# FFN up projection: order of VectorE's and ScalarE's work around the change from whole products to seven block products

## The reference, cut to what matters

```python
def conv_ffn(h, w_up, conv_w, conv_b, w_down):
    u = h @ w_up                                   # 1024 x 5632, f32
    up = pad(u, two rows in front)
    u = sum(up[:, i:i + T] * conv_w[i] for i in range(3)) + conv_b
    gate, val = split(u, 2)                        # 2816 each
    return (gelu(gate) * val) @ w_down
```

## Time and profile before

| what | value |
|---|---|
| median of 3 runs | 2358.38 us (2356.68 to 2360.41) |
| profiled execution, its own time | 2357.89 us |
| span of the profile | 2356.1 us |
| granted TensorE clock, mean | 0.996 of full speed |
| PE busy | 2308.7 us (98%) |
| DVE busy | 1409.2 us (60%) |
| ACT busy | 758.0 us (32%) |
| POOL busy | 918.5 us (39%) |

### The profile page before, as it was taken

The page is one execution under the profiler, slowest core; times in us unless marked ns, Lnnn a source line. Parts: engine busy times, 40 slices in busy tenths (PEclk is TensorE's granted clock), DMA queues, the critical chain, the costliest instruction groups (busy, mean ns, idle before and its releaser), DMA issues.

```text
span 2356.1 us, 33483 instructions
## 1 busy us (share of the span) xinstructions
PE 2308.7 (98%) x12752; PEld 1880.9 (80%) x12752; DVE 1409.2 (60%) x1641; ACT 758.0 (32%) x1253; POOL 918.5 (39%) x545
## 2 busy tenths in 40 slices
PE   7999999999999999999999989999999999999998
PEld 6788888888888888888877867888878887777776
DVE  7755374537543754576538885555541487757775
ACT  4311131112112211334225234444432445114442
POOL 3311231123112214312466467777734445422164
PEclk9999999999999999999999999999999999999999
DMA  3211211121111114664453422222246433211123
GB/s 146 79 54 46 73 54 57 51 73 58 51 55 63 63 54 125 204 200 151 171 161 127 168 89 81 81 81 83 85 164 209 139 123 98 70 59 38 35 81 117
DMA packets 71175, 230.67 MB, mean 98 GB/s; under 512 B 6785, under 2 KB 11009, under 8 KB 70401
## 3 DMA queue, kind: packets, MB, share of 16 engines
q1 hardware_dynamic: 40560, 138.76, 18.2%
q10 hardware_dynamic: 30480, 89.97, 10.4%
HBM read 182.04 MB, written 46.66 MB: 97 GB/s over the span
## 4 chain that ended last, share of the span: by engine, by line
PE 89%; DVE 5%; ACT 2%; issue 1%; POOL 1%; DVEq 1%; DMA 1%; POOLq 1%; ACTq 0%; SPq 0%
PE psg L763 7%; PE psg L768 6%; PE psg L770 6%; PE psg L631 3%; PE psg L636 3%; PE psg L635 3%; PE psa L1235 3%; PE psa L1237 3%; PE psa L1238 3%; PE psb L1237 2%; PE psb L1235 2%; PE psb L1238 2%; PE psg L725 2%; PE psg L728 2%; PE psg L729 2%; PE psa L863 1%
## 5 line engine op out<-in xcount | busy, mean ns | idle before, releaser
L520 POOL CAST whi<-wraw 128x1024 fp32r<-128x1024 f32 (+1 forms) x142 | 158.2, 1114 | 1113.4 <-PE psg L763 516.6
L522 POOL TENSOR_TENSOR wlo<-wraw,whi 128x1024 fp32r<-128x1024 f32 (+1 forms) x142 | 361.4, 2545 | 20.5 <-issue 0.2
L763 PE MATMUL psg<-xhi,whi 128*128 128x512 f32 x640 | 260.9, 408 | 0.0
L770 PE MATMUL psg<-xhi,wlo 128*128 128x512 f32 x640 | 259.5, 406 | 0.0
L768 PE MATMUL psg<-xlo,whi 128*128 128x512 f32 x640 | 257.2, 402 | 0.0
L631 PE MATMUL psg<-xhi,whi 128*128 128x512 f32 x464 | 185.3, 399 | 2.0 <-issue 1.9
L636 PE MATMUL psg<-xhi,wlo 128*128 128x512 f32 x464 | 183.4, 395 | 0.0
L635 PE MATMUL psg<-xlo,whi 128*128 128x512 f32 x464 | 182.8, 394 | 0.0
L595 POOL TENSOR_TENSOR wlo<-wraw,whi 128x1024 fp32r<-128x1024 f32 (+1 forms) x50 | 112.0, 2241 | 146.6 <-ACT whi L2778 78.5
L763 PEld LDWEIGHTS psg<-xhi,whi 128*128 128x128 f32 x640 | 120.9, 189 | 26.8 <-issue 6.3
L770 PEld LDWEIGHTS psg<-xhi,wlo 128*128 128x128 f32 x640 | 120.8, 189 | 22.6 <-issue 1.0
(11 more groups left out here) (706 smaller groups left out, 5992.0 us busy)
## 6 DMA issues: line engine op xcount, KB each, us to landing
wraw<-w SPq DMA_DIRECT2D x206, 512.0 KB, 3.5
later_scratch<-stage ACTq DMA_DIRECT2D x40, 512.0 KB, 2.6
sraw<-w SPq DMA_DIRECT2D x18, 512.0 KB, 4.1
ff_scratch<-ring ACTq DMA_DIRECT2D x10, 512.0 KB, 2.6
ff_scratch<-ff ACTq DMA_DIRECT2D x10, 512.0 KB, 2.6
ff<-ff_scratch ACTq DMA_DIRECT2D x5, 1024.0 KB, 7.0
xres<-xt ACTq DMA_DIRECT2D x4, 1024.0 KB, 11.1
RV<-later_scratch SPq DMA_DIRECT2D x4, 1024.0 KB, 11.3
```

The source lines that it names most:

```text
L520: pool.tensor_copy(whi[:, u, 0:width], wraw[:, u, 0:width])
L522: pool.tensor_tensor(wlo[:, u, 0:width], wraw[:, u, 0:width], whi[:, u, 0:width].bitcast(F32), ALU.subtract).then_inc(w_ready, 1)
L763: mm = pe.matmul(ps[:, cols], whi[:, slot, w_cols], xhi[:, k, cols], start=(k == 0), stop=False)
L770: mm = pe.matmul(ps[:, cols], wlo[:, slot, w_cols], xhi[:, k, cols], start=False, stop=(k == KT - 1))
```

## The change

Arithmetic and outputs stay as they are. What changes:

- DVE's `hidden` is split in `take`, `plain_taps` and `hidden_made`, and the calls are written out. DVE takes pair 4 and makes the last token lows ahead of the taps and the hidden product of pair 3. The taps of pair 4 are made between `gate_first` and `gate_last` of pair 5.
- Pair 4 is taken in place: its scaled raw value stays in `psg`. For pair 5, whose sums went to `psg`, `fg` and `fv` row 1 take that place (`gate_raw`, `value_raw` at `WHOLE`).
- The order of pair 5's sums becomes 22, 11, 12, 21 (`summed`), and its gate taps follow its value taps at once, ahead of the sums of pair 6.
- The copy of the constants to `cp` and its semaphore are gone: operations read them from `prm`. A semaphore `halves_in` takes over the order for pair 1.
- ACT casts the four token highs ahead of P6's high part, keeps P1 right after it, and makes gelu of pair 3 after P5, P7, P4 and P3's high parts and keep P6. Gate of pair 4, the write of pair 3's hidden tile, and value of pair 4 come after keep P7.
- At the start of the down projection ACT makes the high part of the second weight block ahead of that of hidden tile 1, and the last gelu after the fourth hidden tile and weight block.

The diff, cut to its core:

```diff
 def summed(c, i):
-    return 4 * (i - WHOLE) + (22, 11, 21, 12).index(c) + 1
+    order = (22, 11, 12, 21) if i == WHOLE else (22, 11, 21, 12)
+    return 4 * (i - WHOLE) + order.index(c) + 1
...
         def gate_raw(i):
-            return fg[:, 1, :] if i == FT - 1 else psg[0][:, :]
+            return fg[:, 1, :] if i in (WHOLE, FT - 1) else psg[0][:, :]
...
+        def plain_raw(i):
+            if i == 1:
+                return fg2, fv2
+            return (psg[0], psg[1]) if i == WHOLE - 1 else (fg[:, 1, :], fv[:, 1, :])
...
+            def take(i, u):
+                v.drain()
+                v.wait_ge(g_full, T_UP + 2 * i + u + 1)
+                tt(plain_raw(i)[u][:, 0:T], psg[u][:, :], frs[:, :], MUL).then_inc(g_free[u], 1)
+
+            def plain_taps(i):
+                v.drain()
+                for u, buf in enumerate((fg, fv)):
+                    src = plain_raw(i)[u]
+                    v.wait_ge(sem("cv_a"), 2 * i + u + 1)
+                    stt(buf[:, 0, 1:T], src[:, 0:T - 1], conv_col(i, 4 * u + 1), buf[:, 0, 1:T], MUL, ADD)
+                    v.drain()
+                    stt(buf[:, 0, 2:T], src[:, 0:T - 2], conv_col(i, 4 * u), buf[:, 0, 2:T], MUL, ADD
+                        ).then_inc(sem("cv_taps"), 1)
...
-            hidden(3, middle=(1,), between=(2, 3))
-            hidden(4, lows=last_token_lows)
+            take(3, 0)
+            token_sums_of(1)
+            take(3, 1)
+            token_sums_of(2)
+            token_sums_of(3)
+            take(4, 0)
+            take(4, 1)
+            last_token_lows()
...
+            plain_taps(3)
+            hidden_made(3)
+            value_last(WHOLE)
+            gate_first(WHOLE)
+            plain_taps(4)
+            gate_last(WHOLE)
+            hidden_made(4)
+            value_first(WHOLE)
+            taps(WHOLE, 1, fv, value_raw(WHOLE))
+            taps(WHOLE, 0, fg, gate_raw(WHOLE))
...
                     weight_highs(2)
-                gelu(i)
-            weight_highs(3)
-            gate(WHOLE - 1)
-            put_hidden(WHOLE - 2)
+                else:
+                    gelu(i)
+            s.wait_ge(sem("t_raw"), since("t_raw", 4 * kh))
             s.wait_ge(g_full, T_UP + 2 * WHOLE)
             for k in range(kh):
                 act(xhi[:, k, HALF:T], t4raw[:, k, :], CP).then_inc(sem("t_high"), 1)
-            weight_highs(2)
-            value(WHOLE - 1)
+            weight_highs(1)
             keep("P1", WHOLE)
-            weight_highs(2)
-            gelu(WHOLE - 1)
+            weight_highs(4)
             keep("P6", WHOLE)
+            gelu(WHOLE - 2)
             weight_highs(2)
             s.wait_ge(sem("t_low"), since("t_low", 4 * kh))
             keep("P7", WHOLE)
-            weight_highs(1)
+            gate(WHOLE - 1)
+            put_hidden(WHOLE - 2)
+            value(WHOLE - 1)
+            weight_highs(3)
+            gelu(WHOLE - 1)
+            keep("P1", WHOLE + 1)
             put_hidden(WHOLE - 1)
-            keep("P1", WHOLE + 1)
             weight_highs(2)
             value_base(WHOLE)
...
+            s.wait_ge(sem("st_made"), since("st_made", len(PRODUCTS)))
+            weights_high(0, 0, 1)
             s.wait_ge(sem("gate_in"), since("gate_in", FT - WHOLE))
             hidden_high(0, 0, 1)
-            s.wait_ge(sem("st_made"), since("st_made", len(PRODUCTS)))
-            weights_high(0, 0, 1)
             gate_base(FT - 1)
             hidden_high(0, 1, 0)
             weights_high(0, 1, 0)
-            gate_gelu(FT - 1)
             hidden_high(0, 1, 1)
             weights_high(0, 1, 1)
+            gate_gelu(FT - 1)
```

More of the change, by code:

```diff
@@ L357, in gate_raw, with conv_col @@
         def gate_raw(i):
[L358 removed]
+            return fg[:, 1, :] if i in (WHOLE, FT - 1) else psg[0][:, :]
         def value_raw(i):
[L361 removed]
+            return fv[:, 1, :] if i in (WHOLE, FT - 1) else psg[1][:, :]
+        def plain_raw(i):
+            if i == 1:
+                return fg2, fv2
+            return (psg[0], psg[1]) if i == WHOLE - 1 else (fg[:, 1, :], fv[:, 1, :])
+        def conv_col(i, o):
+            return par_col("conv", 8 * i + o)
         dy = at("dy", x_at, [P, KT, T])
@@ L2066, in last_token_lows @@
                     tt(xlo[:, k, HALF:T], t4raw[:, k, :], xhi[:, k, HALF:T].bitcast(F32), SUB).then_inc(sem("t_low"), 1)
-            hidden(0, first=True)
+            plain_taps(0)
+            hidden_made(0)
             for q in range(2, AGAIN):
-                second_halves(q)
-            hidden(1, first=True)
-            hidden(2, between=(0,))
-            hidden(3, middle=(1,), between=(2, 3))
-            hidden(4, lows=last_token_lows)
-            def conv_col(i, o):
-                return par_col("conv", 8 * i + o)
+                second_halves(q).then_inc(sem("halves_in"), 1)
+            plain_taps(1)
+            hidden_made(1)
+            take(2, 0)
+            take(2, 1)
+            token_sums_of(0)
+            plain_taps(2)
+            hidden_made(2)
+            take(3, 0)
[6 more added lines that the diff above has]
+            last_token_lows()
             def value_last(i):
@@ L2114, in taps @@
                     mm.then_inc(sem("gate_taps"), 1)
[L2116 to L2127, removed]
+            plain_taps(3)
[8 more added lines that the diff above has]
+            taps(WHOLE, 0, fg, gate_raw(WHOLE))
+            for i in range(WHOLE + 1, FT):
+                if i > WHOLE + 1:
                     gate_last(i - 1)
@@ L2130, in _ @@
                 value_last(i)
-                if i > WHOLE:
-                    hidden_made(i - 1)
+                hidden_made(i - 1)
                 if i == FT - 1:
@@ L2750, in gate @@
                 s.wait_ge(sem("f_done"), i + 1)
-                s.wait_ge(sem("cp_ready"), i + 1)
                 s.wait_ge(g_free[0], T_UP // 2 + (3 if first else 2 + i))
-                act(fg[:, 0, :], fg2[:, :] if first and i else fg[:, 1, :], IDN, scale=cp[:, 2:3], bias=cp[:, 3:4]
+                if i == 1:
+                    s.wait_ge(sem("halves_in"), 1)
+                act(fg[:, 0, :], plain_raw(i)[0][:, 0:T], IDN, scale=conv_col(i, 2), bias=conv_col(i, 3)
                     ).then_inc(sem("cv_a"), 1)
@@ L2757, in value @@
                 s.wait_ge(g_free[1], T_UP // 2 + (3 if first else 2 + i))
-                act(fv[:, 0, :], fv2[:, :] if first and i else fv[:, 1, :], IDN, scale=cp[:, 6:7], bias=cp[:, 7:8]
+                if i == 1:
+                    s.wait_ge(sem("halves_in"), 2)
+                act(fv[:, 0, :], plain_raw(i)[1][:, 0:T], IDN, scale=conv_col(i, 6), bias=conv_col(i, 7)
                     ).then_inc(sem("cv_a"), 1)
```

21 lines of the change are left out of this document (4 added, 17 removed).

## The result

The changed kernel takes 2335.99 us (median of 4 runs, 2332.53 to 2337.02) against 2357.99 for the kernel before beside it: ratio 0.9903, 95% interval 0.9886 to 0.992. That is 22 us or 0.97% faster, where I had forecast 2.5 us. Some 20 of the 22 us come from a cause that the forecast did not contain: the removed tile `cp` moves other tiles by 32 bytes. The new order of work by itself gave 2.0 us, near the forecast, though not by all the steps that I had worked out.

What follows compares the result with a forecast made beforehand. PE, busy 98% of the span, was taken as the bound; 0 us from the block products' start plus 2.5 us from the down projection's start, off 2358.38, gave 2355.9 us, range 2351.0 to 2359.0.

Steps and rivals of the forecast that it cites:

- part 3: Small edits: removing the copies to cp and their semaphore, on DVE beside PE's work, was put at 0 us.
- my sum: Whole kernel: 0 us from the block products' start plus 2.5 us from the down projection's start, 2355.9 us.
- part 1: Start of the block products, new ACT and DVE order and pairs 4 and 5 moved: 1.7 - 1.8 = 0 us.
- P6 of pair 5: Block products: PE's wait of 9.7 us before it becomes 0.9 us, with no fall of the clock.
- P4 of pair 5, none: Block products: the 2.15 us wait before it goes; P3 of pair 5 then ends 13.5 us ahead, near 1407.0.
- P6 of pair 6, 4.5 us: Block products: a new PE wait of about 4.5 us, until 1411.6, behind POOL's sums and ACT's list.
- P4 of pair 6: Block products: starts at 1430.3 after a new wait of about 6 us, leaving 1.7 us of PE's lead.
- The clock, 1.8 us at P4 of pair 6: Clock falls after the roughly 6 us wait there, costing 1.8 us, bounds 0 and 2.2.
- Collisions: DVE operations with two SBUF inputs delay POOL: 0.85 us each for 11 wide, 0.42 for 5 narrow.
- The tail, 2.5 us: Start of the down projection: waits before second and fourth weight blocks go, 2.5 us saved, bounds 0 and 2.6.
- The rivals: POOL not held up by pair 5, 2351.5 (0.24); no down-projection gain, 2358.4 (0.16); slower from full blocking, 2362.1 (0.10).
- "Faster": Whole kernel: outcome faster by over 0.2%, under 2353.7 us, given chance 0.28.

Runs made afterwards that it cites:

- first experiment: Kernel before, with only cp's 32 bytes taken from an unused part of sm, so xhi, xlo and the arena lie 32 bytes lower: 2336.34 us, ratio 0.9913.
- second experiment: Changed kernel with 32 unused bytes ahead of xhi, so every tile behind is at its old address: 2354.89 us, ratio 0.9993.
- the tail: Kernel before with tiles 32 bytes lower, plus only the change's ACT list at the start of the down projection: 2333.76 us, ratio 0.9902.

## Why the prediction was wrong

**The missing term.** The step that failed is part 3: "The copies to `cp` (0.17 us and a drain each) are on DVE beside PE's work." (One of the five took 1.05 us in the trace, which changes nothing.) I costed the instructions that go, and put the tile that goes at nothing without a reason. The tile's 32 bytes sat ahead of `xhi`, `xlo` and the arena, and their distance to the weights went from 96 to 64 modulo 256. That is 20.6 us (first experiment), some eight times my forecast. The clock has no part in it: 0.996 to 0.997 before, 0.995 to 0.997 with the tiles moved. The rows of before don't show it, but the trace had a hint: the prediction's 0.233 us from one matmul to the next holds for products on x, while those of t1h and sform started every 0.227 us in the same trace. I did not ask where that difference came from.

**The order, against the kernel with the old addresses.** The second experiment measures my sum: forecast 2.5 us, measured 2.0 us with an interval from 0 up. By the traces the agreement is partly luck. The second experiment's kernel is 1.1 us ahead at P1 of pair 5, which the sum did not have; it loses 1.8 us from there to the down projection (346.5 us against 344.7), where part 1 said 0; and it gains 2.8 us in the down projection's first half. Step by step:

- *P6 of pair 5*: forecast a wait of 0.9 us without a fall of the clock. 0.5 us there. In the changed kernel itself it is 1.8 us in both profiles: PE is done with P2 9.2 us earlier than in the second experiment, and POOL's low is there only 7.9 us earlier. The clock fell behind it in one of the two profiles.
- *P4 of pair 5, none*: right, but one step beside it was missed. P1 of pair 6 waits for its low part (2.2 us, and 1.1 in the changed kernel), as POOL's list has P4 and P3 ahead of it while PE's has it first. So PE's lead at the end of P3 of pair 5, counted from P1 of pair 5, was 11.1 us and not 13.5.
- *P6 of pair 6, 4.5 us*: started 28.2 us after P1 of pair 5, forecast 27.6. The wait is shorter (2.6 us), by what was lost before it. The clock fell here too, and P6 took 4.35 us; as forecast, that cost nothing, since PE waits again.
- *P7 of pair 6*: none, as I had it. In the changed kernel, where P6 ran at full clock, there is one of 2.6 us that I had not seen: keep P6 stands behind the value base and gate base of pair 5.
- *P4 of pair 6*: forecast 1430.3 with a wait of about 6 us and ACT's keep P7 ahead of it. POOL's sums of pair 7 ended at 1427.2, forecast 1427.7. Counted from P1 of pair 5, PE is 1.0 us ahead here, and not 1.7. Timeline of the second experiment's PE:

```profile
1429.97 0.76 PE L1244 MATMUL psa<-xhi,whi 128*128 128x512 f32 x1 [5.91 <-ACT sthird L2850]
```

- *The clock, 1.8 us at P4 of pair 6*: P4 and P1 of pair 7 took 5.26 and 3.12 us in that trace in place of 2.8 each, so it cost 2.8 us. With the 1.0 us of lead this is the loss of 1.8. In the changed kernel's own trace the clock is low in the stretches behind the waits before P6 of pair 5 and before P4 of pair 6 (length, PE, PEld, DVE, ACT, POOL busy, clock, DMA, GB/s):

```profile
1381.00:1384.00 3.00, 2.67 (x7) 2.15 (x8) 2.93 (x2) 1.23 (x3) 3.00 (x3) 0.61 0.00 0
...
1420.00:1422.00 2.00, 0.00 (x0) 0.00 (x0) 0.00 (x0) 1.90 (x3) 1.26 (x2) 1.00 0.00 0
1422.00:1425.00 3.00, 2.17 (x5) 1.82 (x6) 1.98 (x3) 1.20 (x3) 2.58 (x3) 0.60 0.00 0
...
1427.00:1430.00 3.00, 3.00 (x15) 2.47 (x14) 1.37 (x2) 1.84 (x2) 2.56 (x2) 1.00 0.35 137
```

- *Collisions*: 2.0 to 2.3 us for each of pair 5's taps, as in the sum. What the change saves for pair 4 it gives back for pair 5. The Trainium skill (SBUF — State Buffer, "Who interferes with whom") states an exclusive lock, and says of VectorE's two-port modes that the other engine is blocked in full. By such a lock each meeting would cost the whole other operation; the new rows again show a pair in 2.0 to 2.3 us where the two alone take 1.28 and 1.3.
- *The tail, 2.5 us*: right in place and about in size (2.6 to 3.1). DVE's low of hidden tile 1, begun beside POOL's operation, took 2.02 us where one alone takes 0.68, and ended 0.56 us after POOL's. That one meeting is what such a lock would give. The margin sufficed.
- *The rivals*: none was it. "Faster" had 0.28, by another mechanism, so that it came true is luck.

Part 1 by itself, forecast near 0, is a loss: 1.8 us on the old addresses by the traces (0.6 by the times, the tail's 2.6 less the 2.0 measured), 2 to 3 us on the new ones. By the times alone both are within what the intervals allow for nothing. What stays open: why the pace goes by the distance of the two tiles in this uneven way, with what period, and why shifting wlo alone costs so little.

## What to carry to other kernels

A diff that removes or adds a small tile moves all tiles behind it. Where TensorE is the bound, compare the number of matmuls in a stretch without waits before anything else, and try a few distances between the moving and the stationary tiles: here the distance alone spread one kernel over 1.3% (2328.5 to 2358.5, the latter one run), some fifteen times the 2.0 us that this new order gave. When a wait on the bounding engine goes, follow the slowest list behind it (here POOL's) to the next products that need it: of 11.1 us of lead at the end of pair 5 in the second experiment, 1.0 was left at the start of the fifth product after it.

## What the runs showed of the hardware

- The start-to-start time of matmuls of 128x128 by 512 columns depends on where in SBUF the two operands lie relative to each other: twelve of them (P4) take 2.720 us at distance 0 and 2.812 at distance 160, modulo 256 bytes, with all tiles shifted together making no difference (2.747 us both times; 32 bytes, one case). It also depends on what ran before: in the kernel before, P6 behind P3 runs at 0.224 to 0.236 us for eight matmuls and then at 0.227.
- The length of a wait alone doesn't decide whether the clock falls to 0.5 of full behind it. In the changed kernel it fell behind the wait of 1.80 us before P6 of pair 5; in a second profile of the same kernel it did not fall behind the same wait, and a wait of 2.15 us left it alone too. The second profile:

```profile
1380.45 0.50 PE L1243 MATMUL psa<-t2h,sform 128*128 128x512 f32 x1 [1.81 <-POOL sform L597]
```

```profile
1381.00:1384.00 3.00, 3.00 (x15) 2.45 (x14) 2.93 (x3) 0.84 (x2) 3.00 (x2) 1.00 0.00 0
```

The first profile, behind the 0.61 of 1381 to 1384 shown above:

```profile
1384.00:1386.00 2.00, 2.00 (x7) 1.55 (x7) 2.00 (x2) 0.03 (x1) 2.00 (x2) 0.73 0.00 0
```

P6 of pair 5 took 4.44 us in the first profile and 2.86 in the second.
